# Strassen passes of a two-FFN trunk: four sums formed in PSUM by accumulation, running sums copied by ScalarE

## The reference

```python
def swiglu(x, w_gate, w_up, w_down):
    return (jax.nn.silu(x @ w_gate) * (x @ w_up)) @ w_down

h = x + 0.5 * swiglu(rmsnorm(x, ffn1_norm), ffn1_w_gate, ffn1_w_up, ffn1_w_down)
p = rmsnorm(h, mix_norm) @ w_in
...                     # S5 state space mixer and short convolution on p
h = h + jnp.concatenate([s_out, c_out], axis=-1) @ w_out
h = h + 0.5 * swiglu(rmsnorm(h, ffn2_norm), ffn2_w_gate, ffn2_w_up, ffn2_w_down)
y = rmsnorm(h, final_norm)
```

## Time and profile before

| | us |
|---|---|
| median of 3 runs | 1816.64 |
| span of the profiled execution, first to last instruction | 1814.7 |
| TensorE busy | 1796.9 (99%) |
| DVE busy | 1089.7 (60%) |
| ScalarE busy | 565.5 (31%) |
| GpSimd busy | 640.3 (35%) |

### The profile page before, as it was taken

One profiled execution on the slowest core, in us unless ns is written; L12 is line 12 of the kernel. 1 busy time (PEld: TensorE's weight loads), 2 busy tenths in 40 slices (PEclk: granted clock), 3 DMA queues, 4 the chain that ended last, 5 costly groups with the idle time before them and its releaser, 6 DMA issues.

```text
span 1814.7 us, 30725 instructions
## 1 busy us (share of the span) xinstructions
PE 1796.9 (99%) x12169; PEld 1783.1 (98%) x12169; DVE 1089.7 (60%) x1870; ACT 565.5 (31%) x1083; POOL 640.3 (35%) x667
## 2 busy tenths in 40 slices
PE   8999999999999999999999999999999999999998
PEld 7999999999999999999999999999999999999998
DVE  6657755564665655823774768556465565655646
ACT  7411332232323232532112455223232322322224
POOL 2687232332333222203994221233233322323321
PEclk9999999999999999999999999999999999999999
DMA  6133111112111111454114401111212111111112
GB/s 171 36 128 105 42 41 53 53 41 61 39 59 47 47 53 40 141 136 114 47 42 127 152 14 52 53 53 42 64 36 60 47 47 53 47 53 48 53 48 94
DMA packets 162464, 119.70 MB, mean 66 GB/s; under 512 B 10210, under 2 KB 156194, under 8 KB 161812
## 3 DMA queue, kind: packets, MB, share of 16 engines
q1 hardware_dynamic: 157012, 110.36, 20.6%
q0 software_dynamic: 832, 5.28, 0.9%
q10 hardware_dynamic: 4480, 2.10, 0.5%
HBM read 102.01 MB, written 15.72 MB: 65 GB/s over the span
## 4 chain that ended last, share of the span: by engine, by line
PE 96%; DVE 2%; ACT 1%; issue 0%; POOL 0%; DVEq 0%; POOLq 0%
PE bank_pair L1002 21%; PE bank_pair L1004 21%; PE bank_pair L1003 21%; PE bank_down L1002 10%; PE bank_down L1004 10%; PE bank_down L1003 10%; DVE HT L2097 1%; DVE XL L2120 1%; PE bank_pair L1385 0%; PE bank_pair L1358 0%; PE bank_pair L1478 0%; PE bank_pair L1377 0%; PE bank_pair L1110 0%; PE bank_down L1152 0%; DVE S L2114 0%
## 5 line engine op out<-in xcount | busy, mean ns | idle before, releaser
L2322 DVE SCALAR_TENSOR_TENSOR HT<-bank_down,HT 128x344 f32<-128x344 f32 (+2 forms) x480 | 245.1, 514 | 334.9 <-PE bank_down L1004 331.8
L1002 PE MATMUL bank_down<-HH,DQH 128*128 128x344 f32 (+2 forms) x924 | 296.8, 321 | 0.0
L1003 PE MATMUL bank_down<-HL,DQH 128*128 128x344 f32 (+2 forms) x924 | 295.1, 319 | 0.0
L1002 PE MATMUL bank_pair<-XHM,U_hi 128*128 128x344 f32 x720 | 230.4, 320 | 1.9 <-issue 1.7
L1004 PE MATMUL bank_pair<-XHM,U_lo 128*128 128x344 f32 x720 | 229.9, 319 | 0.0
L1003 PE MATMUL bank_pair<-XLM,U_hi 128*128 128x344 f32 x720 | 229.6, 319 | 0.0
L2900 POOL TENSOR_TENSOR U_raw<-AST 128x512 f32<-128x512 f32 x36 | 57.2, 1589 | 426.9 <-PE bank_pair L1004 389.7
L1004 PE MATMUL bank_down<-HH,DQ_lo 128*128 128x344 f32 (+2 forms) x624 | 199.4, 320 | 0.0
L1002 PE MATMUL bank_pair<-XH,U_hi 128*128 128x344 f32 x608 | 194.2, 319 | 0.0
L1004 PE MATMUL bank_pair<-XH,U_lo 128*128 128x344 f32 x608 | 194.1, 319 | 0.0
L1003 PE MATMUL bank_pair<-XL,U_hi 128*128 128x344 f32 x608 | 194.0, 319 | 0.0
(11 more groups left out here) (336 smaller groups left out, 4016.6 us busy)
## 6 DMA issues: line engine op xcount, KB each, us to landing
DQ_raw<-in_ffn_w_down SPq DMA_DIRECT2D x52, 256.0 KB, 2.8
U_raw<-in_ffn_w_gate SPq DMA_DIRECT2D x40, 256.0 KB, 3.0
AST<-in_ffn_w_gate SPq DMA_DIRECT2D x40, 256.0 KB, 2.9
U_raw<-in_ffn_w_up SPq DMA_DIRECT2D x40, 256.0 KB, 2.9
AST<-in_ffn_w_up SPq DMA_DIRECT2D x40, 256.0 KB, 2.9
RAW<-in_w_in SPq DMA_DIRECT2D x16, 512.0 KB, 3.9
DQR<-in_ffn_w_down SPq DMA_DIRECT2D x25, 256.0 KB, 2.7
X<-in_x_prompt SPq DMA_DIRECT2D x8, 512.0 KB, 8.8
```

The source lines that it names most:

```text
L1002: pe.matmul(out, wh, xh, start=first, stop=False)
L1003: pe.matmul(out, wh, xl, start=False, stop=False)
L2322: dve.scalar_tensor_tensor(ht, DB[at % 2][:, 0:rows.stop - rows.start], 0.5, ht, ALU.mult, ALU.add).then_inc(pair_free, 1)
```

## The change

M6, M7 and M4 no longer start an accumulation: they are added onto what stands in bank x, and M3 onto M5 in bank v. Bank x so holds M1, then U2 = M1 + M6, then U3 = U2 + M7, then C21 = U3 + M4, with no sum by DVE. ScalarE copies the running sum out three times (after M1, M6 and M7) into the SBUF blocks of C11, C12 and C22. DVE is left with three sums: C11 = copy + M2, C22 = copy of U3 + M5, C12 = copy of U2 + (M5 + M3). C21 is read from PSUM by SiLU or the multiplication. M7 now waits for the copy of M6 in place of U2, M4 for the copy of M7 in place of U3; M3 still waits for C22, V2a for C11. In ScalarE's list the copy of M6 comes before the splits of S1 and S2, that of M7 behind them. The number and order of matmuls is the same.

```diff
-            "M6": (S2, T2, "x", True, True), "M5": (S1, T1, "v", True, True),
-            "M7": (S3, T3, "x", True, True), "V2a": (A21, B13, "y", True, False),
-            "M3": (S4, B22, "v", True, True), "M4": (A22, T4, "x", True, True),
+            "M6": (S2, T2, "x", False, True), "M5": (S1, T1, "v", True, True),
+            "M7": (S3, T3, "x", False, True), "V2a": (A21, B13, "y", True, False),
+            "M3": (S4, B22, "v", False, True), "M4": (A22, T4, "x", False, True),
...
-SUMS = ["U2", "C11", "U4", "U3", "C22", "C12", "C21"]
+COPIES = ["M1", "M6", "M7"]
+ADDED = ("M6", "M7", "M4", "M3")
+SUMS = ["C11", "C22", "C12"]
...
                 if name == "M1" and pairs >= 2:
-                    pe.wait_ge(summed, sum_count(t - 2, "C21"))
+                    pe.wait_ge((silu_done, h_raw)[g], silu_count(p - 1, (1, 1)))
...
                 if name == "M6":
-                    pe.wait_ge(copied, copy_count(t))
+                    pe.wait_ge(copied, copy_count(t, "M1"))
...
                 if name == "M7":
-                    pe.wait_ge(summed, sum_count(t, "U2"))
+                    pe.wait_ge(copied, copy_count(t, "M6"))
                 if name == "V2a":
                     pe.wait_ge(summed, sum_count(t, "C11"))
                 if name == "M3":
                     pe.wait_ge(summed, sum_count(t, "C22"))
                 if name == "M4":
-                    pe.wait_ge(summed, sum_count(t, "U3"))
+                    pe.wait_ge(copied, copy_count(t, "M7"))
...
-            def copy_m1(t):
-                act.wait_ge(products, products_after(t, "M1"))
-                act.activation((gated, hidden)[t % 2](stage(t)[0], (0, 1)), BANK[t % 2]["x"][:, 0:TW], ACT.Copy
+            def copy_sum(t, name, block):
+                act.wait_ge(products, products_after(t, name))
+                act.activation((gated, hidden)[t % 2](stage(t)[0], block), BANK[t % 2]["x"][:, 0:TW], ACT.Copy
                                ).then_inc(copied, 1)
...
                         silu(t, "V1b", "v", (0, 0))
-                        copy_m1(t)
+                        copy_sum(t, "M1", (0, 1))
                         silu_sum(t, "C11", (0, 1))
                         unit_hi(t + 1, A11)
                         quarter_hi(4 * p - 1)
                         unit_hi(t + 1, A12)
+                        copy_sum(t, "M6", (0, 2))
                         unit_hi(t + 1, S1)
                         unit_hi(t + 1, S2)
+                        copy_sum(t, "M7", (1, 2))
                         silu_sum(t, "C22", (1, 2))
...
-                        silu_sum(t, "C21", (1, 1))
+                        silu(t, "M4", "x", (1, 1))
...
                         h_hi2(p, 0)
-                        copy_m1(t)
+                        copy_sum(t, "M1", (0, 1))
                         h_hi2(p, 1)
                         if more:
                             unit_hi(t + 1, A11)
+                        copy_sum(t, "M6", (0, 2))
                         if p != LAST_PAIR[0]:
                             quarter_hi(4 * p + 2)
...
                         if more:
                             unit_hi(t + 1, S1)
                             unit_hi(t + 1, S2)
+                        copy_sum(t, "M7", (1, 2))
                         h_hi2(p, 2)
...
-            def combine(t, name, product, bank, block, dst, after=None):
+            def combine(t, product, copy, bank, block):
                 dve.wait_ge(products, products_after(t, product))
...
+                dve.wait_ge(copied, copy_count(t, copy))
+                at = (gated, hidden)[t % 2](stage(t)[0], block)
+                dve.tensor_tensor(at, BANK[t % 2][bank][:, 0:TW], at, ALU.add).then_inc(summed, 1)
+
+            def c11(t):
+                combine(t, "M2", "M1", "y", (0, 1))
+
+            def c22(t):
+                combine(t, "M5", "M7", "v", (1, 2))
 
             def c12(t):
-                combine(t, "C12", "M3", "v", (1, 0), (0, 2), "U4")
+                combine(t, "M3", "M6", "v", (0, 2))
...
-                            if name == "M6":
-                                u2_c11(t)
+                            if name == "M2":
+                                c11(t)
...
                             if name == "M7":
-                                u4_u3_c22(t)
+                                c22(t)
```

More of the change, by code:

```diff
@@ L222, in sum_count, with copy_count @@
     return earlier(e, 0, len(SUMS)) + len(SUMS) * (n - 2) + SUMS.index(name) + 1
-def copy_count(t):
+def copy_count(t, name):
     e, n = stage(t)
-    return earlier(e, 0, 1) + n - 1
+    return earlier(e, 0, len(COPIES)) + len(COPIES) * (n - 2) + COPIES.index(name) + 1
 def silu_count(p, block):
@@ L999, in _, with product3 @@
         def _(pe):
[L1000 to L1004, removed]
+            def product3(out, wh, wl, xh, xl, first, last, onto=False):
+                pe.matmul(out, wh, xh, start=first, stop=False, skip_group_check=onto)
+                pe.matmul(out, wh, xl, start=False, stop=False, skip_group_check=onto)
+                return pe.matmul(out, wl, xh, start=False, stop=last, skip_group_check=onto)
             def bank_wait(unit, b):
@@ L1286, in ffn_passes @@
                             last = product3(BANK[g][bank][:, 0:TW], UH[k][:, m], UL[k][:, m], xh(e, u)[:, c], xl(e, u)[:, c],
-                                            first and c == 0, final and c == 3)
+                                            first and c == 0, final and c == 3, name in ADDED)
                             if c == 3:
@@ L1298, in banks_of_ffn @@
                 pe.wait_ge(h_raw, 6 * pairs)
-                pe.wait_ge(summed, sum_count(LAST_PASS[e], "C21"))
+                pe.wait_ge(summed, sum_count(LAST_PASS[e], "C12"))
             ffn_passes(0)
@@ L2323, in pair_add @@
                                          ).then_inc(pair_free, 1)
-            def combine(t, name, product, bank, block, dst, after=None):
+            def combine(t, product, copy, bank, block):
                 dve.wait_ge(products, products_after(t, product))
[L2327 to L2341, removed]
+                dve.wait_ge(copied, copy_count(t, copy))
[5 more added lines that the diff above has]
+                combine(t, "M5", "M7", "v", (1, 2))
             def c12(t):
-                combine(t, "C12", "M3", "v", (1, 0), (0, 2), "U4")
-            def c21(t):
-                combine(t, "C21", "M4", "x", (1, 1), (1, 1), "U3")
+                combine(t, "M3", "M6", "v", (0, 2))
             def mul(t, name, bank, block):
@@ L2412, in ffn_passes @@
                             if name == "M4":
-                                c21(t)
                                 unit_lo(t + 1, S2)
@@ L2443, in ffn_passes @@
                                 h_lo2(p, 3)
-                                c21(t)
-                                mul_sum(t, "C21", (1, 1))
+                                mul(t, "M4", "x", (1, 1))
                                 if more:
```

## The result

The changed kernel takes 1832.49 us, the median of 4 runs (1832.18 to 1832.67), against 1816.70 before: a ratio of 1.0087, 95% interval 1.0073 to 1.0102. So it is 0.9% slower, by 15.8 us; forecast were 1831.8 us and 15.2.

A forecast was written before the change was run, and what follows sets the result against it. TensorE's instruction stream was taken to bound the kernel. 16 stalls of 0.95 us at M3 made 15.2 us, span 1814.7 to 1829.9, median 1831.8 us, other terms costed at nothing; 8-in-10 range 1826 to 1838.

The forecast's parts named there:

- What bounds it: Whole kernel: TensorE's instruction stream is the time, busy 1796.9 of 1814.7 us; waits that become late are paid in full.
- 73 us forecast: DVE: four sums of about 0.51 us leave each of 36 Strassen passes, 73 us less, none reaching the end.
- The accumulation costs nothing: TensorE: a product starting without the start flag costs what the others cost; costed at nothing.
- The wait that decides: M3 in 16 odd passes waits for C22, whose copy of M7 queues behind S2's split: 15.2 us.
- M7's wait for the copy of M6: Odd passes: copy ready at about 1380.1, M7 arrives at 1381.17; room 1.1 us, cost nothing.
- The size of the stall: M3 in odd passes: starts 0.84 us late and loses 0.11 behind it, 0.95 us per pass.
- the bounds of 0.72 and 1.10: Stall at M3 per odd pass: lower if the copy starts 0.40 behind the split, upper if after its end.
- rival D: DVE's removed sums do weigh, so the kernel gets faster: at most 1.7 us, 1815; chance 0.07 together with A.
- The cover behind C22: DVE's queue before V1b, odd passes: A12's low part 0.06 us late, 0.85 given back; costed at nothing, at worst 3 us.
- Rival B: Besides M3, M7 or V1b is late too, from DVE's or ScalarE's backlog: 20.8 us, 1837.4; chance 0.13.
- A: M3 isn't held, so no slower: 1816.6, down to 1814.9; chance 0.07 together with rival D.
- C, the clock: TensorE behind M3 in odd passes runs at half clock: 91 us more, 1923; chance 0.02.

The follow-up runs named there:

- experiment 1: Changed kernel with the copy of M7 moved ahead of the split of S2 in odd passes: 1816.0 us, ratio 0.9997 to before.
- experiment 4: Changed kernel with ScalarE making the copy of M7 twice in the 16 odd passes with a next pass: 1840.59 us, ratio 1.0133.
- experiment 2: Changed kernel with the copy of M7 moved ahead of the split of S2 in even passes only: 1832.74 us, ratio 1.0088.
- both mended kernels: Changed kernel with M7's copy ahead of S2's split in odd passes (1816.0 us), or with M5 copied in place of M7 (1815.55 us).
- Experiment 6: Kernel of experiment 1 plus two small scratch additions on DVE at four places of each pass: 1825.34 us, ratio 1.0048.

## Why the prediction was right, step by step

**What bounds it: TensorE, and waits that become late count in full.** Right: 73 us forecast and 82 measured came off DVE, and the kernel became slower. The size of that term was not as worked out: experiment 1 has the same instructions as the changed kernel, and there DVE's busy time is 60.9 us under before, as some of its instructions are longer beside GpSimd's: in the odd pass the multiplication of C22 takes 1.42 us there and 0.52 in the changed kernel, the low parts of S1 and A11 2.37 and 1.29.

**The accumulation costs nothing.** Right, by experiment 1.

**The wait that decides, and where.** Right: M3, in 16 odd passes, released by C22, that by the copy of M7, that queued behind S2's split (experiments 1 and 4); none in the even passes (experiment 2). M7's wait for the copy of M6 stayed covered, as worked out: the copy ends at 1389.90, M7 starts at 1391.03, room 1.1 us.

**The size of the stall.** Forecast 0.84 + 0.11 = 0.95, measured 1.00 + 0.08. Against the forecast, term by term: the copy started 0.54 behind S2's split (0.52 said) and took 0.44 (0.46); ScalarE to DVE took 0.10 (1395.05 to 1395.15), not 0.03; C22 took 0.52 (0.51); DVE to TensorE took 0.14 (1395.67 to 1395.81), not 0.05; the matmuls behind the first lost 0.08, not 0.11. The two hand-overs are what was undersized, by 0.16 together; they were read from rows 5 and 8, where one was from GpSimd to ScalarE and the other between different instructions. The total of 1.08 a pass lies inside the bounds of 0.72 and 1.10, near the upper.

**16 times 1.08 is 17.3, and 15.8 came.** The difference is mostly a gain that the sum did not have. In the kernel before, TensorE shows no idle time in these passes, yet the third pair tile started late in 16 even passes, those that follow an odd Strassen pass; after the change and in experiment 1 it does not. The kernel before:

```profile
1396.58 0.32 PE L1004 MATMUL bank_pair<-XHM,U_lo 128*128 128x344 f32 x1
1396.74 0.38 PE L1002 MATMUL bank_down<-HH,DQH 128*128 128x344 f32 x1
1396.96 0.32 PE L1003 MATMUL bank_down<-HL,DQH 128*128 128x344 f32 x1
```

and experiment 1:

```profile
1396.24 0.32 PE L1006 MATMUL bank_pair<-XHM,U_lo 128*128 128x344 f32 x1
1396.40 0.32 PE L1004 MATMUL bank_down<-HH,DQH 128*128 128x344 f32 x1
1396.56 0.32 PE L1005 MATMUL bank_down<-HL,DQH 128*128 128x344 f32 x1
```

The step from the tile's first matmul to its second was 0.22 us and became 0.16. What the tile waits for (`pair_tile` waits for `pair_free`) is DVE's addition of the tile two before it. DVE's additions (x2), then the load of the tile's first weight, in the kernel before:

```profile
1396.07 0.93 DVE L2322 SCALAR_TENSOR_TENSOR HT<-bank_down,HT 128x344 f32<-128x344 f32 x2
...
1396.70 0.19 PEld L1002 LDWEIGHTS bank_down<-HH,DQH 128*128 128x128 f32 x1
```

and the additions in experiment 1:

```profile
1395.17 1.00 DVE L2329 SCALAR_TENSOR_TENSOR HT<-bank_down,HT 128x344 f32<-128x344 f32 x2
```

Before, the first addition ends at about 1396.6 and the load starts at 1396.70, 0.12 later than the even spacing of the loads would have it; in experiment 1 the first addition is over by about 1395.7, with TensorE at the tile at 1396.40. There are 16 such tiles and not 18, as I had written ahead of experiment 1: 16 times 0.06 is 1.0 us. Set beside each other matmul by matmul, the traces give 17.0 us for the 16 stalls (1.06 each) and 1.0 back at these tiles, 16.0 together, against 15.8 measured. So rival D existed, at about 1 us. The times alone do not settle it: both mended kernels have a span of 1813.9 in the profile against 1814.7, but the differences of their medians from before, 0.6 and 0.96, lie inside of the intervals.

That the forecast of 15.2 came within 0.6 us of the result is in part luck. The stalls were 1.8 us larger in sum than forecast, and the gain of 1.0 us, which was costed at nothing, took more than half of that back.

**The cover behind C22.** I feared that A12's low part would be 0.06 us late, and gave 0.85 back for the multiplication that no longer runs beside GpSimd's S3. It did take 0.52 (1395.70), and the low parts of S1 and A11 after it took 1.29 in place of 2.37, which I had not foreseen. DVE in the changed kernel, these two and then A12's:

```profile
1397.16 1.29 DVE L2315 TENSOR_TENSOR U_lo<-U_raw,U_hi 128x512 fp32r<-128x512 f32 x2
...
1401.43 0.68 DVE L2315 TENSOR_TENSOR U_lo<-U_raw,U_hi 128x512 fp32r<-128x512 f32 x1
```

A12's low part ended at 1402.11, and V1b came 48 matmuls after M3, at 1403.43: 1.3 us of room, where 0.3 had been. Rival B didn't come. Experiment 6 shows that the fear had its reason: V1b is one of the places that stall with a later queue. With the copy in its better place (experiment 1) the room at V1b is again 0.3 us, as before the change.

**The other rivals.** A is out by 16 waits. C, the clock at half rate behind the stalls, is out: the granted clock is 1.00 in both stretches. By the rule of the Trainium skill weighed in the prediction (TensorE: Matmul & The Clock Gate, "A second HAM failure mode: psum-queue depth-cycling") it could have swung; in this trace it did not: stalls of 1 us, 65 us apart, left it at 1.00.

## What to carry to other kernels

When a result that the bottleneck engine waits for moves to another engine, its price is not its duration but what stands ahead of it in that engine's list, with that instruction's own wait. Write down for each such wait the time at which the bottleneck arrives and the earliest time of the releaser with the whole queue before it; here the 33 us of copies cost nothing and the place of one of them cost 16 us, which moving one line gave back. Work taken off an engine with slack pays mainly in cover, and shows in the time only where the cover had already run out: the lighter DVE gave back 1 us here. Idle time alone does not show such places; the gaps between the starts of matmuls do.

## What the runs showed of the hardware

A hand-over between engines where the later one already sits waiting took 0.10 us from ScalarE to DVE and 0.14 from DVE to TensorE in this chain (0.09 and 0.15 in experiment 4), against 0.03 to 0.05 in the rows that I had taken.

DVE's subtractions and multiplications of two SBUF operands grow beside GpSimd: the multiplication of C22 took 1.37 us in rows 6, and 0.52 in the profile after. It started at 1384.43, GpSimd's S3 ended at 1385.42, and 1385.42 + 0.52 is 0.14 from the 1385.80 at which it ended: it looks like a wait for the rest of S3 rather than a slower pace. Experiment 1 has the same picture: 1.42 us, from 1384.03, where S3 ended at 1385.09. The Trainium skill (SBUF — State Buffer, "SBUF: two separate sides") says that such a DVE instruction and a GpSimd one that reads SBUF share a port pair, and that whichever starts first holds it for its whole instruction while the other waits; the trace agrees, within that 0.14. The sum that reads one operand from PSUM took 0.50 to 0.52 with or without GpSimd beside it. So a shift of a microsecond on one engine changes which instructions meet, and with it their durations, which a sum of fixed durations doesn't see: the low parts of S1 and A11 took 1.29, 2.37 or 3.48 us.
